# Two slots of modulation products in every second head, and one turn of their four rows

## The chip, the cores and the metric

The kernel runs on one core of a Trainium2 chip. Its time is the device time of one execution in microseconds, the median of several runs. The engines run side by side and meet at semaphores only: TensorE multiplies, VectorE (DVE) and ScalarE (ACT) work element by element and take results out of PSUM, GpSimd (POOL) takes a part of the element-wise work, and SyncE (SP) issues the transfers from the chip's memory, which 16 DMA engines carry out.

## The reference

256 tokens of width 1024, in fp32, pass through two blocks one after the other:

```
first block:  x += pool_mixer(rmsnorm(x));                     x += swiglu(rmsnorm(x))   # FFN1
              x += attention(rmsnorm(x), 16 heads of 64) @ w_o; x += swiglu(rmsnorm(x))  # FFN2
              x  = rmsnorm(x)
second block: mod = silu(c) @ ada_w + ada_b          # one row of 1024 times 1024 x 6144
              sh1, sc1, g1, sh2, sc2, g2 = split(mod, 6)
              h  = rmsnorm(x) * (1 + sc1) + sh1;  x += g1 * (mixed(h) @ w_out)
              h2 = rmsnorm(x) * (1 + sc2) + sh2;  x += g2 * moe_ffn(h2)
              x  = rmsnorm(x)
```

`mixed` joins a sparse attention of 8 heads and a recurrent branch; `moe_ffn` has 64 experts of width 256. The change bears on how `mod` is computed. It depends on the input `c` alone, so it can be done anywhere ahead of the second block; the kernel does its products inside the 16 heads of the first attention.

## The kernel before, in words

The program is one stream of instructions for each engine, written out by hand. Activations lie with features on partitions, as 8 chunks of 128 x 256 tokens. All weights but the experts' come as 93 slots of 128 x 3072 fp32 (1.5 MB) through a ring of 11 places in SBUF. SP loads slot n (L443 to L469; in this stretch L457) once the semaphore `w_used` says that the slot that had its place eleven before has been used. It issues in the order of the slots, on one queue. Slots 0 to 21 belong to FFN1, 22 to 29 to keys, values and queries (`S_KVQ`), 30 to 45 to the modulation (`S_ADA`), 46 to 48 to the output projection (`S_O`), 49 to 70 to FFN2 (`S_FFN2`).

**First attention** (`attention`, L610, on TensorE). Iteration j does the scores of head j (L618, L619), turns the softmax weights of head j-2 for the product with the values (L625, three transposes), calls `between(j)`, and multiplies the values of head j-3 (L635, L636). DVE adds the bias to the scores and takes the maximum (L1473 to L1480), ScalarE takes the exponential (L1142, L1143), DVE divides (L1485 to L1487), ScalarE copies the turned weights out of PSUM (L1150), and after every second head the result (L1154). On DVE the scores of head j come before the division of head j-1.

**Modulation** (`modulation`, L654). `between` is `modulation`: in each of the 16 heads it waits for one slot (128 rows of `ada_w` by 3072 columns) and does its six products of one column of silu(c) with 512 columns (L661). The 6144 results lie as twelve pieces of 512 in PSUM banks 5 to 7, four pieces in a bank, in rows 0, 32, 64 and 96: piece j is in bank 5 + j // 4, row 32 * (j % 4), and `tile_position=(0, r)` puts its matmul on the strip of 32 columns of the array that writes there. A fp32 matmul is two passes and shows as two records. Pieces add up over eight chunks of `c`, which are two slots each.

**Output projection** (L705): 64 matmuls of 128 x 256, 128 records. Then the **turning**. ScalarE has copied the four rows to SBUF (`modrow`), each by a copy of its own (L1208). 48 matmuls with one row of one element as the moving operand (L718) turn them, so that feature n of `mod` lies on partition n % 128. The sum of squares for FFN2's norm (`norm_sum(3)`, L558) stands after the second row of four. ScalarE then takes the root (L1105) and DVE the reciprocal (L1431); DVE adds `ada_b` to the turned columns (`modulation_columns`, L1566), and this releases TensorE (`mod_ready`) to clear FFN2's banks (L564) and to start FFN2 (L579 to L581). While the turning goes on, DVE and ScalarE add the last parts of the projection to x, split them into two parts each (L1100, L1101, L1429), and take their squares (L1102).

**The rest**: FFN2, the projections and branches of the second block (with a second attention of 8 heads by the same function, without `between`), and the experts, whose weights come by 64 loads of 3 MB.

Of the kernel before, what the change touches and what calls it, by code (L numbers as in the profile page):

```python
# [11 lines left out]
ALU = mybir.AluOpType  # L12
ACT = mybir.ActivationFunctionType
# [4 lines left out]
P = 128  # L18
# [6 lines left out]
HEADS_1, HEADS_2, HEAD = 16, 8, 64  # L25
# [52 lines left out]
VEC = {}  # L78
# [63 lines left out]
def build(nc, xT, vec, consts, selector, inv_count, pool_w, ws, rel, lora, router, router_bias, experts, out):  # L142
# [3 lines left out]
    with ExitStack() as ctx:  # L146
# [11 lines left out]
        vecs = sb("vecs", [P, N_VEC])  # L158
        con = sb("con", [P, N_CONST])
        ones = sb("ones", [P, P])  # L160
# [4 lines left out]
        mod = sb("mod", [P, 48])  # L165
# [226 lines left out]
        O2_PARTS, RW_PARTS, MIXED_PARTS = 5 * KC, 5 * KC + AC, 6 * KC  # L392


        def mod_products(q):
            return B[(4, 5, 0, 7)[q]][:, 0:12]

        PROJ_BANKS = [B[4], B[5], B[7]]
        U_V1, U_K1, U_Q1 = 0, 8, 16
# [149 lines left out]
        def _(pe):  # L549
# [3 lines left out]
            def norm_sum(k, bank=B[6], weights=lambda c: ones[:]):  # L553

                for g in range(4):
                    pe.wait_ge(sq_ready, SQ_BASE[k] + g + 1)
                    for c in (2 * g, 2 * g + 1):
                        mm = nc.tensor.matmul(bank[:, 0:T], weights(c), sq[:, c, :], start=(c == 0), stop=(c == KC - 1))  # L558
                mm.then_inc(ss_ready, 1)
# [94 lines left out]
            def modulation(n):  # L654
# [7 lines left out]
                                          skip_group_check=True, tile_position=(0, r))  # L662
                mm.then_inc(w_used, 1)


            pe.wait_ge(const_loaded, 16)
            norm_sum(2)
# [27 lines left out]
            pe.sem_inc(w_used, 8)  # L695
            pe.wait_ge(proj_used, U_Z)
            pe.wait_ge(csil_ready, 1)
            attention(HEADS_1, 0, q1, k1, v1, ex, pts, B[4:5], between=modulation)
            pe.wait_ge(o_copied, HEADS_1 // 2)
            for i in range(24, 32):  # L700
                dc = i - 24
# [6 lines left out]
            pe.wait_ge(res_ready, 4)  # L708
            pe.sem_inc(w_used, 3)

            pe.wait_ge(mod_copied, 4)
            for q in range(4):
                if q == 2:
                    norm_sum(3)
                for j in range(3):
                    for t in range(4):
                        row = slice(32 * q, 32 * q + 1)
                        mm = nc.tensor.matmul(mod_products(q)[:, 4 * j + t:4 * j + t + 1], modrow[row, j, t * P:(t + 1) * P], ones[row, 0:1], start=True, stop=True)  # L718
            mm.then_inc(mod_turned, 1)

            pe.wait_ge(mod_ready, 1)
            ffn(S_FFN2, 3, FFN_CHUNKS)
# [362 lines left out]
        def _(act):  # L1085
# [118 lines left out]
            attention(HEADS_1, 0, h, ex, pts, B[4:5])  # L1204

            act.wait_ge(w_used, S_O)
            for q in range(4):
                nc.scalar.activation(modrow[32 * q:32 * q + 1, :, :], banks[32 * q:32 * q + 1, 5:8, :], ACT.Copy).then_inc(mod_copied, 1)  # L1208
            ffn_start(S_FFN2)
            norm_squares(3, "norm_ffn1")  # L1210

# [185 lines left out]
        def _(dve):  # L1397
# [67 lines left out]
            def attention(heads, n0, bias, extra, ex):  # L1465
                for j in range(heads + 1):
                    if j < heads:
                        b, e, k = B[j % 2], ex[:, j % 3, :], 2 * (j % 3)
                        dve.wait_ge(s_ready, n0 + j + 1)

                        if j >= 3:
                            dve.wait_ge(pt_ready, n0 + j - 2)
                        nc.vector.scalar_tensor_tensor(e[:, 0:T], b[:, 0:T], HEAD ** -0.5, bias[:, j, :], ALU.mult, ALU.add)  # L1473
                        m = nc.vector.scalar_tensor_tensor(e[:, T:T + P], b[:, T:T + P], HEAD ** -0.5, bias[:, j, P:T], ALU.mult, ALU.add)
                        m.then_inc(s_used, 1)
                        dve.wait_ge(s_used, n0 + j + 1)
                        if extra is not None:
                            then(nc.vector.tensor_tensor(e, e, extra, ALU.add))
                        nc.vector.tensor_reduce(nmax[:, k:k + 1], e[:, 0:T], AX_X, ALU.max, negate=True)
                        nc.vector.tensor_reduce(nmax[:, k + 1:k + 2], e[:, T:T + P], AX_X, ALU.max, negate=True).then_inc(max_ready, 1)  # L1480
                    if j >= 1:
                        a = j - 1
                        e, k = ex[:, a % 3, :], 2 * (a % 3)
                        dve.wait_ge(exp_ready, n0 + a + 1)
                        then(nc.vector.reciprocal(rrec[:, k:k + 2], rsum[:, k:k + 2]))  # L1485
                        nc.vector.tensor_scalar(e[:, 0:T], e[:, 0:T], rrec[:, k:k + 1], None, ALU.mult)
                        nc.vector.tensor_scalar(e[:, T:T + P], e[:, T:T + P], rrec[:, k + 1:k + 2], None, ALU.mult).then_inc(p_ready, 1)  # L1487
# [78 lines left out]
            def modulation_columns():  # L1566
                dve.wait_ge(mod_turned, 1)
                by_row = lambda a: a.rearrange("p (j q t) -> p j q t", j=3, q=4)
                for q in range(4):
                    ins = nc.vector.tensor_tensor(by_row(mod[:])[:, :, q, :], mod_products(q).rearrange("p (j t) -> p j t", j=3), by_row(vecs[:, VEC["ada_b"][0]:VEC["ada_b"][1]])[:, :, q, :], ALU.add)  # L1570
                ins.then_inc(mod_ready, 1)
                dve.wait_ge(mod_ready, 1)
                for dst, col, g in ((scale1, 8, "norm1_g"), (scale2, 32, "norm2_g")):
                    last = nc.vector.scalar_tensor_tensor(dst[:], mod[:, col:col + 8], 1.0, vecs[:, VEC[g][0]:VEC[g][1]], ALU.add, ALU.mult)
                then(last)
# [437 lines left out]
```

## Time and profile before

| | us |
|---|---|
| median of 3 runs (lowest, highest) | 1533.23 (1532.24, 1540.92) |
| the profiled execution's own time | 1534.7 |
| its span in the profile | 1533.0 |
| TensorE busy, share of the span | 1420.4, 93% |
| VectorE busy | 718.2, 47% |
| ScalarE busy | 500.4, 33% |
| GpSimd busy | 171.5, 11% |
| DMA mean over the span | 236 GB/s |

The span is cut into 40 slices of 38.3 us. The first attention starts at 318 us, in the ninth slice, and FFN2 at 428, in the twelfth. In the slices from the ninth to the twelfth the page gives 280, 424, 395 and 95 GB/s of transfers. The modulation products are 192 matmul records at L661, the turning 96 at L718. A busy share says how long an engine had work in it, not that this work set the end; for that one reads the chain of waits, followed back from the last instruction, and then each stretch by itself.

### The profile page before, as it was taken

What the parts mean: (1) busy time and instruction counts of PE and PEld (TensorE: products, weight loads), DVE (VectorE), ACT (ScalarE), POOL (GpSimd) and SP (SyncE); (2) the same over time, 40 slices, a digit from 0 to 9 for tenths busy, and PEclk for the clock granted to TensorE, in tenths of its full rate; (3) what the DMA queues carried; (4) which work ended last, traced back from release to release, by engine and by line L of the source; (5) the groups of instructions that cost most, each with busy time, mean ns of one, the idle gap of its engine ahead of it and who ended that gap; (6) DMA issues with size and microseconds to landing.
All of it is one profiled execution on the core that took longest, in us unless ns stands there. A gap on an engine that the chain in (4) does not pass through costs nothing.

```text
span 1533.0 us, 25786 instructions
## 1 busy us (share of the span) xinstructions
PE 1420.4 (93%) x10983; PEld 1109.9 (72%) x10986; DVE 718.2 (47%) x1188; ACT 500.4 (33%) x809; POOL 171.5 (11%) x76
## 2 busy tenths in 40 slices
PE   4999997999999999799798877979999999999996
PEld 3999997954899999698695877845554545555453
DVE  5766656444266665689894537331112112211213
ACT  2533324434333342456334133221222222222221
POOL 0000000000000000376670024300000000000000
PEclk7999999999999999899896998889999999999998
DMA  9754552269925445113305042429889999999990
GB/s 362 312 201 165 179 191 83 56 280 424 395 95 190 181 168 199 44 43 125 120 5 247 3 167 83 173 99 396 342 343 407 426 425 425 422 424 426 420 376 28
DMA packets 36166, 362.16 MB, mean 236 GB/s; under 512 B 3955, under 2 KB 5107, under 8 KB 7412
## 3 DMA queue, kind: packets, MB, share of 16 engines
q1 hardware_dynamic: 35364, 358.50, 58.5%
q0 software_dynamic: 720, 2.46, 0.8%
q8 instruction: 65, 1.06, 0.3%
q14 instruction: 17, 0.14, 0.0%
HBM read 358.25 MB, written 2.69 MB: 235 GB/s over the span
## 4 chain that ended last, share of the span: by engine, by line
PE 84%; DVE 13%; ACT 1%; issue 1%; DMA 0%; POOL 0%; DVEq 0%; SPq 0%; ACTq 0%
PE banks L1018 14%; PE banks L579 12%; PE banks L580 12%; PE banks L581 12%; PE banks L1047 7%; PE banks L978 4%; PE banks L986 4%; PE banks L558 2%; DVE scr L1640 2%; PE banks L661 2%; PE banks L705 2%; DVE ring L1629 1%; PE banks L844 1%; PE banks L635 1%; PE banks L618 1%
## 5 line engine op out<-in xcount | busy, mean ns | idle before, releaser
L1018 PE MATMUL banks<-ring,scr 128*64 128x512 f32 x1024 | 225.4, 593 | 0.7 <-ACT scr L1349 0.7
L579 PE MATMUL banks<-h_hi,gu_hi 128*128 128x256 f32 x704 | 200.0, 284 | 0.0
L580 PE MATMUL banks<-h_lo,gu_hi 128*128 128x256 f32 x704 | 199.5, 283 | 0.0
L581 PE MATMUL banks<-h_hi,slot_lo 128*128 128x256 f32 x704 | 199.4, 283 | 0.0
L1018 PEld LDWEIGHTS banks<-ring,scr 128*64 128x64 f32 x1024 | 73.1, 137 | 145.6 <-issue 144.7
L579 PEld LDWEIGHTS banks<-h_hi,gu_hi 128*128 128x128 f32 x704 | 135.5, 192 | 0.4 <-issue 0.3
L580 PEld LDWEIGHTS banks<-h_lo,gu_hi 128*128 128x128 f32 x704 | 135.4, 192 | 0.1
L581 PEld LDWEIGHTS banks<-h_hi,slot_lo 128*128 128x128 f32 x704 | 135.4, 192 | 0.0
L1888 DVE TENSOR_TENSOR out_lo<-banks,out_hi 128x512 fp32r<-128x512 f32 x64 | 44.2, 691 | 194.2 <-ACT out_hi L1375 194.2
L581 PE MATMUL banks<-slot_lo,slot_lo 128*128 128x256 f32 x416 | 118.9, 286 | 0.0
L1047 PE MATMUL banks<-ring,scr 128*64 128x512 f32 x512 | 116.9, 598 | 0.9 <-ACT scr L1369 0.9
L1876 DVE TENSOR_TENSOR scr<-banks,scr 128x256 f32<-128x256 f32 x32 | 13.6, 424 | 198.8 <-ACT scr L1362 198.8
L579 PE MATMUL banks<-act_hi,down_hi 128*128 128x256 f32 x352 | 99.9, 284 | 4.1 <-DVE slot_lo L1414 4.1
L1414 DVE TENSOR_TENSOR slot_lo<-ring,gu_hi 128x2048 fp32r<-128x2048 f32 x44 | 100.6, 2291 | 3.0 <-ACT gu_hi L1116 3.0
L580 PE MATMUL banks<-act_lo,down_hi 128*128 128x256 f32 x352 | 99.6, 283 | 0.0
L581 PE MATMUL banks<-act_hi,slot_lo 128*128 128x256 f32 x352 | 99.6, 283 | 0.0
L1128 ACT ACTIVATE scr<-scr 128x256 f32<-128x256 f32 x44 | 18.4, 418 | 240.1 <-DVE scr L1446 240.1
L517 POOL TENSOR_TENSOR slot_lo<-ring,win_hi 128x1024 fp32r<-128x1024 f32 x20 | 48.6, 2433 | 369.8 <-ACT win_hi L1218 369.8
L1362 ACT ACTIVATE scr<-banks 128x256 f32<-128x256 f32 x32 | 12.3, 383 | 209.9 <-PE banks L1018 209.9
L581 PEld LDWEIGHTS banks<-slot_lo,slot_lo 128*128 128x128 f32 x416 | 80.7, 194 | 0.0
L1116 ACT ACTIVATE gu_hi<-ring 128x2048 fp32r<-128x2048 f32 x42 | 79.5, 1898 | 3.2 <-PE banks L718 3.2
L1047 PEld LDWEIGHTS banks<-ring,scr 128*64 128x64 f32 x512 | 33.9, 136 | 60.1 <-issue 54.8
(381 smaller groups left out, 3150.0 us busy)
## 6 DMA issues: line engine op xcount, KB each, us to landing
ring<-ws SPq DMA_DIRECT2D x93, 1536.0 KB, 7.5
ring<-experts SPq DMA_DIRECT2D x64, 2048.0 KB, 10.2
ring<-experts SPq DMA_DIRECT2D x64, 1024.0 KB, 9.7
ring<-experts SPq DMA_DIRECT2D x1, 3072.0 KB, 11.4
scr<-bias_line POOLq DMA_DIRECT2D x4, 512.0 KB, 8.8
bias_line<-scr SPq DMA_DIRECT2D x1, 1536.0 KB
x<-xT SPq DMA_DIRECT2D x1, 1024.0 KB, 5.0
scr<-pool_w SPq DMA_DIRECT2D x1, 1024.0 KB, 7.7
```

Of the source, the lines that this page charges most:

```text
L517: nc.gpsimd.tensor_tensor(dst, src, hi.bitcast(F32), ALU.subtract).then_inc(win_w_lo, 1)
L558: mm = nc.tensor.matmul(bank[:, 0:T], weights(c), sq[:, c, :], start=(c == 0), stop=(c == KC - 1))
L579: nc.tensor.matmul(out, hi, move_hi, start=start, stop=False, skip_group_check=True)
L580: nc.tensor.matmul(out, hi, move_lo, start=False, stop=False, skip_group_check=True)
L581: return nc.tensor.matmul(out, lo, move_hi, start=False, stop=stop, skip_group_check=True)
L978: mm = nc.tensor.matmul(bank[:, c * 4 * CAP:(c + 1) * 4 * CAP], tok[:, tb, kc * P:(kc + 1) * P], pick[q % 2][:, tb, :], start=(n == 0 and ...
L986: mm = nc.tensor.matmul(B[c // 2][:, c % 2 * T:c % 2 * T + T], part[:, c * P:(c + 1) * P], spread[k % 2], start=False, stop=False, skip_gr ...
L1018: mm = nc.tensor.matmul(B[4][CAP * j:CAP * (j + 1), :], hs[:, c, CAP * u:CAP * (u + 1)], unit(u)[:, c * 512:(c + 1) * 512], start=(c == 0) ...
L1047: mm = nc.tensor.matmul(B[6 + half][CAP * j:CAP * (j + 1), :], act_pt[:, f, CAP * j:CAP * (j + 1)], unit(u)[:, lo:lo + 512], start=(f == 0 ...
L1116: nc.scalar.activation(dst, slot(base + s)[:, lo:hi], ACT.Copy).then_inc(signal, 1)
L1414: nc.vector.tensor_tensor(slot_lo[PLACE[base + s]][:, lo:to], slot(base + s)[:, lo:to], hi.bitcast(F32), ALU.subtract).then_inc(signal, 1)
L1888: ins = nc.vector.tensor_tensor(out_lo[part], B[6 + half], out_hi[part].bitcast(F32), ALU.subtract)
```

## The change

It does three things. `two_modulations` does nothing in even heads and the products of two slots, one after the other, in odd heads; since banks 5 to 7 are then copied with rows in them that no product writes, three matmuls with zeros fill them first. The four row copies on ScalarE become one, of partitions 0 to 96. The 48 turning matmuls become 12: each has 97 rows of 128 columns as weights and as moving operand the columns 0, 32, 64 and 96 of the identity, so that it picks four rows at once and writes four neighbouring columns of bank 4. The sum of squares comes after the turning, and one addition on DVE takes the place of four.

```diff
--- before.py
+++ after.py
@@ -392,8 +392,8 @@
         O2_PARTS, RW_PARTS, MIXED_PARTS = 5 * KC, 5 * KC + AC, 6 * KC
 
 
-        def mod_products(q):
-            return B[(4, 5, 0, 7)[q]][:, 0:12]
+        mod_products = B[4][:, 0:48].rearrange("p (j t q) -> p j q t", j=3, t=4)
+        mod_rows = slice(0, 3 * 32 + 1)
 
         PROJ_BANKS = [B[4], B[5], B[7]]
         U_V1, U_K1, U_Q1 = 0, 8, 16
@@ -662,6 +662,11 @@
                                           skip_group_check=True, tile_position=(0, r))
                 mm.then_inc(w_used, 1)
 
+            def two_modulations(head):
+                if head % 2:
+                    modulation(head - 1)
+                    modulation(head)
+
 
             pe.wait_ge(const_loaded, 16)
             norm_sum(2)
@@ -695,7 +700,9 @@
             pe.sem_inc(w_used, 8)
             pe.wait_ge(proj_used, U_Z)
             pe.wait_ge(csil_ready, 1)
-            attention(HEADS_1, 0, q1, k1, v1, ex, pts, B[4:5], between=modulation)
+            for b in range(5, 8):
+                nc.tensor.matmul(B[b], zeros[:, 0:P], zeros[:], start=True, stop=False, skip_group_check=True)
+            attention(HEADS_1, 0, q1, k1, v1, ex, pts, B[4:5], between=two_modulations)
             pe.wait_ge(o_copied, HEADS_1 // 2)
             for i in range(24, 32):
                 dc = i - 24
@@ -708,15 +715,12 @@
             pe.wait_ge(res_ready, 4)
             pe.sem_inc(w_used, 3)
 
-            pe.wait_ge(mod_copied, 4)
-            for q in range(4):
-                if q == 2:
-                    norm_sum(3)
-                for j in range(3):
-                    for t in range(4):
-                        row = slice(32 * q, 32 * q + 1)
-                        mm = nc.tensor.matmul(mod_products(q)[:, 4 * j + t:4 * j + t + 1], modrow[row, j, t * P:(t + 1) * P], ones[row, 0:1], start=True, stop=True)
+            pe.wait_ge(mod_copied, 1)
+            for j in range(3):
+                for t in range(4):
+                    mm = nc.tensor.matmul(mod_products[:, j, :, t], modrow[mod_rows, j, t * P:(t + 1) * P], ident[mod_rows, 0:P:32], start=True, stop=True)
             mm.then_inc(mod_turned, 1)
+            norm_sum(3)
 
             pe.wait_ge(mod_ready, 1)
             ffn(S_FFN2, 3, FFN_CHUNKS)
@@ -1204,8 +1208,7 @@
             attention(HEADS_1, 0, h, ex, pts, B[4:5])
 
             act.wait_ge(w_used, S_O)
-            for q in range(4):
-                nc.scalar.activation(modrow[32 * q:32 * q + 1, :, :], banks[32 * q:32 * q + 1, 5:8, :], ACT.Copy).then_inc(mod_copied, 1)
+            nc.scalar.activation(modrow[mod_rows, :, :], banks[mod_rows, 5:8, :], ACT.Copy).then_inc(mod_copied, 1)
             ffn_start(S_FFN2)
             norm_squares(3, "norm_ffn1")
 
@@ -1566,8 +1569,7 @@
             def modulation_columns():
                 dve.wait_ge(mod_turned, 1)
                 by_row = lambda a: a.rearrange("p (j q t) -> p j q t", j=3, q=4)
-                for q in range(4):
-                    ins = nc.vector.tensor_tensor(by_row(mod[:])[:, :, q, :], mod_products(q).rearrange("p (j t) -> p j t", j=3), by_row(vecs[:, VEC["ada_b"][0]:VEC["ada_b"][1]])[:, :, q, :], ALU.add)
+                ins = nc.vector.tensor_tensor(by_row(mod[:]), mod_products, by_row(vecs[:, VEC["ada_b"][0]:VEC["ada_b"][1]]), ALU.add)
                 ins.then_inc(mod_ready, 1)
                 dve.wait_ge(mod_ready, 1)
                 for dst, col, g in ((scale1, 8, "norm1_g"), (scale2, 32, "norm2_g")):
```

## Rows read from the trace of the kernel before

**Rows 1.** The page, chain that ended last: shares of the span.
```profile
PE 84%; DVE 13%; ACT 1%; issue 1%; DMA 0%; POOL 0%; DVEq 0%; SPq 0%; ACTq 0%
```

**Rows 2.** Windows, TensorE: from:to length, busy (records), granted clock, DMA share, GB/s.
```profile
330.11:361.58 31.47, 31.47 (x186) 1.00 1.01 426
377.31:381.08 3.77, 3.68 (x23) 1.00 1.03 434
```

**Rows 3.** Chain of waits, one head: start, duration, engine, tile, line, count.
```profile
373.38 0.58 PE banks L635 x2
373.96 0.22 PE banks L636 x2
374.17 0.63 PE banks L618 x2
374.80 0.22 PE banks L619 x2
375.02 0.48 PE banks L625 x3
375.50 1.81 PE banks L661 x12
```

**Rows 4.** Timeline, TensorE's weight loads in one head: start, duration, [idle before].
```profile
325.09 0.10 PEld L661 LDWEIGHTS banks<-ring,small 128*1 128x1 f32 x8 [0.17 <-issue]
325.52 0.09 PEld L661 LDWEIGHTS banks<-ring,small 128*1 128x1 f32 x2 [0.33 <-issue]
...
326.90 0.29 PEld L618 LDWEIGHTS banks<-scr 64*128 64x128 f32 x2 [0.86 <-issue]
```

**Rows 5.** Line L457, slot loads: issue, and time to landing of first and last.
```profile
L457 SPq DMA_DIRECT2D ring<-ws x24: 332/333/2305, 318.2 to 377.5; - x24
...
DMA to landing us min/median/max: 7.8/7.8/7.8
...
DMA to landing us min/median/max: 33.3/33.3/33.3
```

**Rows 6.** Timeline, DVE in one head: scores taken up, last scaling.
```profile
327.86 0.42 DVE L1473 SCALAR_TENSOR_TENSOR scr<-banks,scr 128x256 f32<-128x256 f32 x1 [1.21 <-PE banks L619]
...
329.50 0.28 DVE L1487 TENSOR_SCALAR scr<-scr,small 128x128 f32<-128x128 f32 x1
```

**Rows 7.** Timeline, row copies on ScalarE and the output projection.
```profile
381.62 5.82 ACT L1208 ACTIVATE scr<-banks 1x1536 f32<-1x1536 f32 x4
...
381.77 27.89 PE L705 MATMUL banks<-scr,ring 128*128 128x256 f32 x128 [0.47 <-ACT scr L1154]
```

**Rows 8.** Chain of waits, from the projection's end to FFN2.
```profile
409.82 5.07 PE banks L718 x48
414.88 5.33 PE banks L558 x16
...
425.35 0.41 DVE mod L1570 x4
...
426.21 1.48 PE banks L564 x3
```

**Rows 9.** Windows, TensorE, columns as in group 2: the two falls of the clock.
```profile
414.96:418.37 3.41, 3.41 (x9) 0.50 1.01 425
425.20:428.61 3.41, 2.44 (x10) 0.50 0.00 0
```

**Rows 10.** Timeline, last square on ScalarE, reciprocal on DVE.
```profile
413.42 0.61 ACT L1102 ACTIVATE scr<-x 128x512 f32<-128x512 f32 x1
...
420.76 1.75 DVE L1431 RECIPROCAL rinv<-rt 128x256 f32<-128x256 f32 x1 [6.33 <-ACT rt L1105]
```

**Rows 11.** Windows, TensorE: a gap later in the kernel and what followed.
```profile
854.60:857.70 3.10, 0.01 (x2) 1.00 0.00 0
858.70:862.10 3.40, 3.40 (x71) 0.50 0.02 5
```

**Rows 12.** Windows, TensorE: a stretch of the second attention.
```profile
825.00:838.00 13.00, 12.70 (x38) 0.50 0.36 152
```

## The prediction, written before the result was known

> **What bounds the kernel now.** I read the chain of waits first: TensorE holds 84% of it [rows 1], and around the change all of it. The change touches the stretch from 318 us, where the first attention starts, to 428 us, where the second feed-forward (FFN2) is under way, so I read that stretch closely: first as windows, then head by head.
>
> In the windows TensorE is never idle while the heads run, at full granted clock, while the 16 DMA engines are as busy as they can be: share 1.01, 426 GB/s [rows 2]. So two resources are full at once, and an edit that relieves only TensorE gets only what the DMA lets through.
>
> The chain shows one head: values 0.58 + 0.22, scores 0.63 + 0.22, turning the weights 0.48, modulation 1.81 us [rows 3], a period of 3.93 us. Modulation is 46% of it. Its weight loads start in a burst of eight, then after 0.43 us a pair, and one more pair as much later [rows 4]. Each 1x512 fp32 matmul is two passes; four matmuls on the four column strips share the array. Six matmuls in one slot are thus a wave of four and a wave of two, at two passes of about 0.43 us each: 4 x 0.43 = 1.71, plus 0.10 before the array is free.
>
> The weights arrive on a schedule of their own. After 318.2 us 24 slots are issued; the first (modulation slot 3, since 0 to 2 were already there) lands after 7.8 us, at 326.0, the 24th (issued 377.5) after 33.3 us, at 410.8 [rows 5]. That is 84.8 / 23 = 3.69 us a slot, for demand every 3.93. Slot 15 is the 13th: 326.0 + 12 x 3.69 = 370.3 us, and before it is wanted at 375.5 [rows 3].
>
> **The change, part by part.**
>
> *Two slots in one place.* Twelve matmuls on four strips are three full waves: 6 x 0.43 + 0.10 = 2.67 us in place of 2 x 1.81 = 3.62. Two heads then need 2 x (0.80 + 0.85 + 0.48) + 2.67 = 6.93 us on TensorE in place of 7.86. Is anything else late first? The scores' matmuls begin at 326.90 [rows 4]; DVE takes them up 0.96 us later, at 327.86, and has then scaled the weights of the head before by 329.50 + 0.28 = 329.78 [rows 6], 2.88 us after the matmuls' start. In the new even-to-odd step TensorE comes to the turning of the weights 0.85 + 0.48 + 0.80 + 0.85 = 2.98 us after the even head's scores began; DVE is ready at 2.9. It just fits. Only in the first pair, where there are no values yet, does TensorE wait some 0.7 us.
>
> TensorE alone: scores of heads 0 and 1 after the new zero matmuls end at 320.8, first pair to 323.5, scores, turning, scores, the 0.7 us wait and turning to 326.9; six more periods bring the last pair to 326.9 + 6 x 6.93 = 368.5, its end to 371.1. From the end of the last modulation to the output projection it is 381.77 - 377.31 = 4.46 us [rows 3, 7]; start at 375.6.
>
> The DMA: two slots need 7.38 us, more than 6.93. From the fourth pair on the odd slot is late, and its six matmuls then run alone. For the last: 370.3 + 1.8 + 4.5 = 376.6. The later of the two counts, **376.6 instead of 381.8: 5.1 us won** (6.2 if the DMA did not bind). The projection's own slots land at 374.0, 377.7 and 381.4, each before its use (the third of its 27.9 us [rows 7] begins 21 us in). Slots are given back up to 2.9 us later, but eleven are outstanding, so the queue stays full. The three issues that wait for the projection's end come while the queue still drains, and FFN2 has eight slots in hand by then.
>
> *Zeros into banks 5 to 7.* Three 128x512 bf16 matmuls. The nearest row is the same form before FFN2: the stretch of 1.48 us at half clock [rows 8, 9], so about 0.2 us each at full clock, 0.65 in all (at most 1.5). It is on TensorE's path, but lies before the stretch in which the DMA sets the pace; that covers it. Without this cover it costs the 0.65 that I put into the 375.6.
>
> *One row copy.* ScalarE's four copies hold 381.62 to 387.44 [rows 7]; one is a quarter, since only the partitions are more. 4.4 us less, hidden beside the projection: it only has to precede its end. Worth nothing. The split of FFN2's first slot comes after it, but waits for a slot that lands at 326.0 + 16 x 3.69 = 385.0.
>
> *Turning in twelve matmuls.* Before: 48 records (24 matmuls of two passes) in 5.07 us, twice, with the sum of squares (5.33) between them [rows 8]. One record is 0.106 us. Now 24 records. No row has 97 rows and four moving columns; below stands 0.106 (1 row, 1 column), above 0.16 (turning the weights, 128 rows and 128 moving columns, 0.48 / 3 [rows 3]): 2.5 to 3.8 us. I take 2.5, as four columns are far nearer to one than to 128. The Trainium skill (TensorEngine Tiling, Instruction Overhead) says a matmul with one moving column lasts as long as one with sixty; that would give the same 2.5, and no run here shows it.
>
> *The sum of squares comes last.* Counted from the projection's end (409.68): turning ends at +2.7. The last square is written at 414.03 = +4.35 [rows 10]; the three parts ahead of it take till +5.3, so it isn't waited for. At full clock 16 records of 0.218 (the projection's 27.9 / 128 [rows 7], same shape) are 3.5 us: end at **+6.2, before +10.5**. But the reciprocal, which lay beside the second turning, is now on the path. After the sum: the reciprocal starts 0.54 later (420.76 after 420.21) and takes 1.75 [rows 10]; then one addition of 0.2 in place of 0.41, and 0.45 till the first clearing matmul (426.21 after 425.76) [rows 8]: TensorE idles **2.9 us** and begins to clear at +9.1 (before +16.5). FFN2's second slot is split by ScalarE and DVE beside its first, as before.
>
> *The clock.* Before, the granted clock fell from its upper level to half (2.4 to 1.2 GHz) after five microseconds of turning, at 415, for about 3.4 us, and again at the end of the second turning [rows 9]. The first made the sum of squares 1.9 us longer, the second the clearing 0.7 (1.48 against 0.75) and FFN2, which began at 427.69, 0.5. Now turning is short, but 2.9 us of idleness follows. A gap of 3.10 us elsewhere was followed, a microsecond after work resumed, by 3.4 us at 0.50 [rows 11]: 1.7 us lost. Without a fall FFN2 runs at full rate from +9.85 against an effective +18.5: 8.6 won. With it: 6.9, with a longer one 5.2. I take **7.3**, between.
>
> **Sum**: 5.1 + 7.3 = 12.4 us. The profiled execution took 1534.7 (span 1533.0 and 1.7 around it); 1522.3 there. The median of the runs shown is 1533.2, 1.5 lower: 1520.8, so 1521. What follows FFN2 is started by TensorE's or DVE's progress and moves along.
>
> **The rivals.**
>
> *A, the waves don't cross the slots.* If the wait or the semaphore between two slots keeps the second's matmuls out of the half-full wave, a pair costs 3.62, and the zeros and the first wait lie open: the projection starts at 383.2, 1.4 us later than before. With the turning: 12.4 - 6.5 = 5.9 won, 1527. For it: no burst in the trace crosses a slot. Against it: with the slot landed, nothing in between holds the queue, and records go out four at a time [rows 4].
>
> *B, neither DMA nor clock takes its part.* 6.2 + 8.6 = 14.8, 1518.4. For it: the gap is 2.9, shorter than the one that was followed by a fall. Against it: the landings are counted and stood in queue throughout.
>
> *C, slower: the clock falls during attention.* Even steps have no modulation any more; 4.3 us of scores, turning and values lie between pairs, in place of 2.1. The second attention, which has none at all, ran at 0.50 for 13 us on end [rows 12]. If the first falls to half in an even step and stays there, a pair costs 13.9 instead of 7.86, 8 x 6.0 = 48 us more, with the turning gain left: 1534.7 + 48 - 7.3 - 1.5 = 1574. Two pairs at half eat up the gain; from about four on the kernel is over 1% slower (12.4 + 15.3 = 27.7, at 13.9 - 7.4 = 6.5 each). Against it: 3.77 us without modulation at the end of attention kept 1.00 [rows 2], and with it the granted clock stayed up into the projection. The Trainium skill (TensorE: Matmul & The Clock Gate, Part 4: PE-mode transpose) has it that transposes don't count as work for the clock; by that rule the even steps are poorer still than they look. The trace shows that they suffice for 3.8 us.
>
> **Numbers.** Forecast 0.63, A 0.12, B 0.2, C 0.05. The range takes in A and B and the spread of the clock: 1516.5 to 1528; the forecast alone 1518.5 to 1523.5. A measurement of this kernel can tell 1% (15.3 us) from nothing; 1517.9 is the line. The far side of B passes it, a bit over half of its 0.2: faster 0.12. Slower: C, 0.05. Same: 0.83.
>
> **What would show it.** After: eight groups of 24 modulation records, the first three 2.67 us long, and from the fourth on 1.81 twice with a gap before the second that ends with a landing; the projection's start near 376.6; turning x24 in 2.5; the sum of squares in 3.4; then 2.9 us idle for the reciprocal. Wrong if the pair takes 3.6, if the projection starts after 379, if the granted clock in the heads is below 1.00, or if FFN2 starts less than 6 us closer to the projection's end.

## The result, and the profile after

The kernel before and the changed one ran in turn on one chip, eleven executions each. The medians are 1531.73 us (1530.4 to 1540.92) and 1527.82 us (1520.37 to 1532.45); the ratio is 0.9945, 95% interval 0.9926 to 0.9964. That is faster, by less than 1%, and 6.8 us above the forecast of 1521. The two profiled executions say something else: 1534.7 before, 1523.15 after (span 1521.5), 11.55 us apart where the forecast had 12.4. Two gaps are to be explained: 12.4 against 11.55, and 11.55 in the profiles against 3.9 between the medians. In what follows, "a profile" is the one profiled execution of a run, and a run's own time is the median of its executions.

The stretches, from one first matmul to the next (us):

| | before | after | won | forecast |
|---|---|---|---|---|
| start to the first scores | 318.44 | 318.04 | 0.4 | 0 |
| first scores to projection | 63.33 | 57.35 | 6.0 | 5.1 |
| projection to FFN2 | 45.36 | 40.02 | 5.3 | 7.3 |
| FFN2 to the last instruction | 1105.90 | 1106.07 | -0.2 | 0 |

The shares of the chain of waits hardly move against [rows 1]:

```profile
PE 83%; DVE 14%; ACT 1%; issue 1%; DMA 0%; DVEq 0%; SPq 0%; ACTq 0%
```

**The heads.** The chain of waits of the kernel after, two heads in place of the one of [rows 3] (start, duration, engine, tile, line, count; the second head's values, scores and turning left out):

```profile
340.55 2.69 PE banks L661 x24
343.24 0.58 PE banks L635 x2
343.81 0.22 PE banks L636 x2
344.03 0.63 PE banks L618 x2
344.66 0.22 PE banks L619 x2
344.88 0.48 PE banks L625 x3
...
347.47 2.69 PE banks L661 x24
```

Twenty-four records take 2.69 us, and the period of a pair is 6.92. The weight loads of such a pair, from the timeline of TensorE's loads (start, duration, line, shape, count, [idle before]), against [rows 4]:

```profile
340.48 0.10 PEld L661 LDWEIGHTS banks<-ring,small 128*1 128x1 f32 x8 [0.17 <-issue]
340.91 0.10 PEld L661 LDWEIGHTS banks<-ring,small 128*1 128x1 f32 x4 [0.33 <-issue]
341.34 0.10 PEld L661 LDWEIGHTS banks<-ring,small 128*1 128x1 f32 x4 [0.33 <-issue]
```

After the first eight, four come every 0.43 us, where before they were two: the second slot's matmuls take the places that the first slot's last wave leaves empty.

**From the projection to FFN2**, the chain of waits after, against [rows 8]:

```profile
403.29 0.14 issue
403.43 2.81 PE banks L721 x24
406.24 5.26 PE banks L558 x16
...
411.53 0.48 ACT rt L1109
...
412.03 1.76 DVE rinv L1434
...
413.82 0.22 DVE mod L1572
414.04 0.45 issue
414.49 1.49 PE banks L564 x3
```

TensorE clears at +11.2 us from the projection's end (403.29), not at +9.1. The line of L558 shows why: the sum of squares takes 5.26 us, almost what it took before. The windows of TensorE (from:to, length, busy and records, granted clock, DMA share, GB/s) give the reason, and two windows of the heads beside them:

```profile
324.90:328.30 3.40, 3.40 (x18) 0.50 1.00 426
330.00:361.00 31.00, 31.00 (x203) 1.00 1.01 426
406.80:410.20 3.40, 3.40 (x9) 0.50 1.00 417
413.60:417.00 3.40, 2.52 (x9) 0.50 1.02 430
```

The clock falls to half (1.2 GHz) 0.6 us after the sum of squares begins, for 3.4 us, and again before the clearing: two falls, as before [rows 9]. It also fell once in the heads, and then stayed up.

**The row copy** on ScalarE, from its timeline, against [rows 7]: a quarter, as counted, and beside the projection.

```profile
375.23 1.44 ACT L1211 ACTIVATE scr<-banks 97x1536 f32<-97x1536 f32 x1
```

### The profile page after: what moved, and what is told of

Its sections match the earlier page's. It is cut to its first block, busy times and chain, and to the rows that moved or that the text cites. A ratio compares the mean times of both kernels' runs of the same rounds, so it can differ in the third digit from the quotient of the medians.

```text
span 1521.5 us, 25641 instructions
## 1 busy us (share of the span) xinstructions
PE 1406.1 (92%) x10913; PEld 1100.9 (72%) x10917; DVE 720.0 (47%) x1185; ACT 495.3 (33%) x806; POOL 171.6 (11%) x76
## 3 DMA queue, kind: packets, MB, share of 16 engines
HBM read 358.25 MB, written 2.69 MB: 237 GB/s over the span
## 4 chain that ended last, share of the span: by engine, by line
PE 83%; DVE 14%; ACT 1%; issue 1%; DMA 0%; DVEq 0%; SPq 0%; ACTq 0%
PE banks L1022 14%; PE banks L579 12%; PE banks L581 12%; PE banks L580 12%; PE banks L1051 8%; PE banks L982 4%; PE banks L990 4%; DVE scr L1642 2%; PE banks L558 2%; PE banks L712 2%; PE banks L661 2%; DVE ring L1631 1%; PE banks L848 1%; PE banks L635 1%; PE banks L569 1%
## 5 line engine op out<-in xcount | busy, mean ns | idle before, releaser
L579 PE MATMUL banks<-h_hi,gu_hi 128*128 128x256 f32 x704 | 200.0, 284 | 0.0
L581 PE MATMUL banks<-h_hi,slot_lo 128*128 128x256 f32 x704 | 199.4, 283 | 0.0
L579 PEld LDWEIGHTS banks<-h_hi,gu_hi 128*128 128x128 f32 x704 | 135.5, 193 | 0.4 <-issue 0.3
L581 PEld LDWEIGHTS banks<-h_hi,slot_lo 128*128 128x128 f32 x704 | 135.4, 192 | 0.0
L581 PE MATMUL banks<-slot_lo,slot_lo 128*128 128x256 f32 x416 | 118.9, 286 | 0.0
L579 PE MATMUL banks<-act_hi,down_hi 128*128 128x256 f32 x352 | 99.9, 284 | 4.1 <-DVE slot_lo L1417 4.1
L581 PE MATMUL banks<-act_hi,slot_lo 128*128 128x256 f32 x352 | 99.6, 283 | 0.0
L581 PEld LDWEIGHTS banks<-slot_lo,slot_lo 128*128 128x128 f32 x416 | 80.7, 194 | 0.0
```

The source lines that it names most:

```text
L579: nc.tensor.matmul(out, hi, move_hi, start=start, stop=False, skip_group_check=True)
L581: return nc.tensor.matmul(out, lo, move_hi, start=False, stop=stop, skip_group_check=True)
```

## The experiments

The expectations of the first runs speak of theories by number. Theory 1: the spread of the changed kernel's times is the clock in the heads. Theory 2: it arises after FFN2 begins. Theory 3, formed after the third run: it is code that TensorE has to fetch again, ahead of everything that the change touches.

In the diffs below `...` stands for lines left out.

**e1_pairs**: the pairs alone, on the kernel before.

```diff
+            def two_modulations(head):
+                if head % 2:
+                    modulation(head - 1)
+                    modulation(head)
...
-            attention(HEADS_1, 0, q1, k1, v1, ex, pts, B[4:5], between=modulation)
+            attention(HEADS_1, 0, q1, k1, v1, ex, pts, B[4:5], between=two_modulations)
```

> The kernel before with the two slots in every second head and nothing else (no zeros, four row copies, 48 turning matmuls). Both theories: a pair of slots in 2.67 us where the second slot has landed, the projection's start near 376, so 5 to 6 us less in the profiled execution: 1527 against a median of 1532. Theory 1 (the wide spread of the changed kernel, 1520 to 1532, comes from the granted clock, which falls in the heads without modulation in a part of the executions): this kernel shows the spread too, some executions hardly under 1531, and a fall of the clock between 318 and 375 in the profile or none at all, as it comes. Theory 2 (the spread comes from something after FFN2 starts, set off by the earlier start of FFN2): about half of the spread or none.

Measured: 1529.67 us, 12 executions (1523.6 to 1536.82), ratio 0.9976 [0.9956, 0.9997]. In its profile (1523.6) the projection starts 58.04 us after the first scores, 5.3 less than before. Here the landings can be seen to set the pace. Groups of modulation records in its chain, the fifth to the seventh:

```profile
345.20 3.14 PE banks L661 x24
...
352.58 3.12 PE banks L661 x24
...
359.94 3.14 PE banks L661 x24
```

Their starts lie 7.37 us apart, two slots at 3.69, not 6.92. And within one such group, TensorE's weight loads:

```profile
359.87 0.10 PEld L661 LDWEIGHTS banks<-ring,small 128*1 128x1 f32 x8 [0.17 <-issue]
360.30 0.09 PEld L661 LDWEIGHTS banks<-ring,small 128*1 128x1 f32 x2 [0.33 <-issue]
360.73 0.09 PEld L661 LDWEIGHTS banks<-ring,small 128*1 128x1 f32 x2 [0.34 <-issue]
361.20 0.10 PEld L661 LDWEIGHTS banks<-ring,small 128*1 128x1 f32 x6 [0.38 <-DMA ring<-ws]
```

The first slot's last wave goes on with two records at a time, since the second slot isn't there; then a landing releases the rest. The clock did not fall in these heads.

**e2_turn**: the changed kernel with the old distribution over the heads (the zeros stay).

```diff
-            attention(HEADS_1, 0, q1, k1, v1, ex, pts, B[4:5], between=two_modulations)
+            attention(HEADS_1, 0, q1, k1, v1, ex, pts, B[4:5], between=modulation)
```

> The changed kernel with one slot in each head, as before the change; zeros, one copy, twelve turning matmuls and the late sum of squares stay. The projection starts near 382.3 (0.6 for the zeros), FFN2 starts 12.7 us after its end in place of 18.0: 1527 in the profiled execution. Theory 1: executions close together, within 2 us, like the kernel before. Theory 2: spread over 8 us like the changed kernel.

Measured: 1529.71 us, 12 executions (1523.75 to 1538.46), 0.9975 [0.9951, 0.9999]. The spread is as wide without the pairs, so theory 1 falls. In its profile heads to projection take 63.33 us, the time of before to the hundredth, and projection to FFN2 39.89. The chain after the projection:

```profile
416.14 2.81 PE banks L721 x24
418.95 5.26 PE banks L558 x16
```

The turning's gain and the slow sum of squares are there whatever happens in the heads. The two parts add up: 5.3 (e1_pairs) and 5.5 (45.36 - 39.89) are 10.8 of the 11.3 that both stretches win in the profile of after.

**e3_repeat**: the changed kernel once more, nothing edited.

> The changed kernel once more, word for word, to see another of its executions: 1520 to 1532. Theory 1: where the profiled execution takes 1527 or more, its clock is at half for more than 3.4 us between 318 and 375; where it takes 1521, for less. Theory 2: the stretch from 318 to FFN2's start is the same within 1 us in both and the difference of 5 us lies behind it.

Measured: 1521.38 us, 6 executions (1518.39 to 1530.22), 0.9912 [0.9884, 0.994]. The profile caught the 1530.22. Neither theory held: heads 57.05, projection to FFN2 40.03, both as in the other profile. The difference is that its first scores come at 325.35 us and not at 318.04. The windows of TensorE in FFN1, first after (1523.15), then e3_repeat:

```profile
139.00:144.00 5.00, 5.00 (x44) 1.00 0.85 332
144.00:149.00 5.00, 5.00 (x44) 1.00 0.12 49
```

```profile
139.00:144.00 5.00, 0.43 (x2) 0.68 0.85 292
144.00:149.00 5.00, 4.79 (x26) 0.64 0.31 124
```

and the place where e3_repeat stands still, in its timeline of TensorE:

```profile
138.45 0.28 PE L581 MATMUL banks<-act_hi,slot_lo 128*128 128x256 f32 x1
143.56 0.55 PE L579 MATMUL banks<-h_hi,gu_hi 128*128 128x256 f32 x1 [4.84 <-issue]
```

TensorE stands 4.84 us for "issue", which is no wait on another engine, exactly where FFN1's loop branches back to its first instruction (L581 to L579). Then the clock is at half for a few microseconds. The page's section on DMA queues has the missing piece, packets, MB and share, first after, then e3_repeat:

```profile
q8 instruction: 65, 1.06, 0.3%
```

```profile
q8 instruction: 74, 1.21, 0.3%
```

Nine packets more of code, 0.15 MB, and 7.3 us to the first scores. And these nine lie in the loop's second turn. The DMA view of e3_repeat for 122 to 234 us has this line:

```profile
q8 instruction: 9, 0.15, 0.6%
```

The same view of after has no packet on queue q8. Two of the nine fall between 138 and 144 us, where TensorE stands still, the other seven in the turn after it. That is theory 3. Of the profiles so far, e2_turn (1533.63) has 74 packets and a standstill of 5.41 us at the same branch; before, after and e1_pairs have 65 and none.

Read with this, the times of the changed kernel fall into two groups: after and e3_repeat together have ten executions between 1518.39 and 1524.98, median 1521.65, and seven from 1527.82 to 1532.45, median 1528.33. The kernel before, over 62 executions on four chips (those of all runs up to e10_after_unroll), has 39 up to 1534.1 with a median of 1531.36 and 23 from 1535.89 with 1538.2. Group against group the change is worth 9.7 and 9.9 us. On the fifth chip, that of e11_before_unroll_again and e12_before_unroll_two, its 23 executions go from 1528.55 to 1542.24 without an empty stretch between (four lie from 1535.16 to 1535.43), so for the kernel before the border between the groups is not a sharp one.

**e4_bank7**: the turned columns go to bank 7, which FFN2 doesn't use at first, so TensorE no longer waits for DVE's addition before it clears and starts FFN2.

```diff
-        mod_products = B[4][:, 0:48].rearrange("p (j t q) -> p j q t", j=3, t=4)
+        mod_products = B[7][:, 0:48].rearrange("p (j t q) -> p j q t", j=3, t=4)
...
-            pe.wait_ge(mod_ready, 1)
             ffn(S_FFN2, 3, FFN_CHUNKS)
+            pe.wait_ge(mod_ready, 1)
```

> The changed kernel with the turned columns in bank 7 in place of 4, and TensorE's wait for mod_ready behind FFN2 instead of ahead of it. FFN2 no longer waits for the reciprocal and the addition: 2.9 us of idleness go, and with it one fall of the clock may go. Expected 3 us under the changed kernel on the same chip, up to 5 if the clock stays up; 0 if the wait is taken over by another (the split of the last part of x, DVE's L1432, ends before).

Measured: 1518.66 us, 6 executions (1517.15 to 1527.71), 0.9909 [0.9877, 0.9941]; the profile is of the 1517.15. Heads 57.31, projection to FFN2 36.61, 3.4 less than after. The chain:

```profile
403.25 2.81 PE banks L721 x24
406.06 5.25 PE banks L558 x16
411.31 0.86 PE banks L564 x4
412.17 0.12 PE banks L579
```

The gap of 3.0 is gone, and with it the second fall (clearing 0.86, FFN2's first record 0.12 in place of 0.21). The first fall stays: 5.25. So the gap for the reciprocal does not bring about the slow sum of squares: the first fall comes without the second.

**e5_order**: e4_bank7, and the twelve turning matmuls stand in the middle of the sum of squares.

```diff
-            def norm_sum(k, bank=B[6], weights=lambda c: ones[:]):
+            def norm_sum(k, bank=B[6], weights=lambda c: ones[:], midway=None):
...
+                    if g == 2 and midway is not None:
+                        midway()
...
-            norm_sum(3)
+            norm_sum(3, midway=turn_rows)
```

> The kernel with the turned columns in bank 7, and the twelve turning matmuls put between the second and the third part of the sum of squares, where TensorE would else wait for the squares. Theory a (it is the low work of 2.8 us of turning in one piece right ahead of the sum that costs the clock): from the projection's end to the end of the sum 6.3 us in place of 8.2, no fall there, 1.9 us less than with bank 7 alone. Theory b (any such turning costs the clock wherever it stands): the fall stays, the time is that of bank 7 within 0.5 us.

Measured: 1522.78 us, 6 executions (1513.85 to 1524.58), 0.9894 [0.9863, 0.9926]. The profiled 1522.7 is one of the upper group (74 packets, a standstill of 5.54 us at FFN1's branch), but its stretch can be read: projection to FFN2 34.93, another 1.7 less. Chain, then the window of TensorE:

```profile
412.11 1.97 PE banks L560 x8
414.08 2.58 PE banks L724 x24
416.65 1.83 PE banks L560 x8
418.49 0.05 issue
418.54 0.81 PE banks L566 x3
```

```profile
411.80:420.00 8.20, 8.00 (x51) 1.00 1.01 425
```

The same work, 40 records, takes 6.38 us in place of 8.07, without a fall. That this is the doing of the order is likely, but the next run takes from the proof.

**e6_half**: of each of the 16 modulation slots only half is loaded, and the products use that half twice, so half of `ada_w` is left out. TensorE's work is the same. (The slot number has to be known ahead for this, so three turns of SP's loop of slot loads are written out.)

```diff
-                    sp.dma_start(slot(s), ws[RING * i + s]).then_inc(landed[s], 16)
+                    n = RING * i + s
+                    cols = SLOT // 2 if isinstance(i, int) and S_ADA <= n < S_O else SLOT
+                    sp.dma_start(slot(s)[:, 0:cols], ws[n][:, 0:cols]).then_inc(landed[s], 16)
...
-                    mm = nc.tensor.matmul(B[5 + j // 4][r:r + 1, :], csil[:, c:c + 1], w[:, b * 512:(b + 1) * 512], start=(c == 0), stop=(c == KC - 1),
+                    mm = nc.tensor.matmul(B[5 + j // 4][r:r + 1, :], csil[:, c:c + 1], w[:, b % 3 * 512:(b % 3 + 1) * 512], start=(c == 0), stop=(c == KC - 1),
```

> The changed kernel with half of each modulation slot loaded and used (columns 0 to 1535 twice; the other half of ada_w is left out). Theory of the forecast (from the fourth or fifth pair on the second slot's landing sets the pace): no group of modulation records lasts more than 2.7 us, all eight pairs come every 6.92 us, from the first scores to the projection 56.3 us at full clock in place of 57.3. Rival (TensorE, DVE or the code sets the pace there and the landings only coincide): groups of 3.05 us every 7.38 us stay, 57.3.

Measured: 1523.28 us, 6 executions (1521.7 to 1525.64), 0.9915 [0.9891, 0.9939]. Its profile (1524.93) has the 74 packets and a standstill of 5.34 us at FFN1's branch, so the whole time says little; the stretch is what counts. Every group takes 2.69 and they come 6.92 apart to the end. Two of them, late in the chain:

```profile
354.36 2.69 PE banks L669 x24
...
361.28 2.69 PE banks L669 x24
```

Heads to projection 55.71, against 57.05 to 57.43 in seven profiles with the whole loads: the transfers cost the change 1.6 us. In this profile the clock did not fall in the sum of squares:

```profile
410.31 2.81 PE banks L729 x24
413.13 3.57 PE banks L566 x16
...
419.51 0.81 PE banks L572 x3
```

```profile
410.30:420.00 9.70, 6.86 (x44) 1.00 0.89 341
```

So 3.57 us is the price at full clock. The second fall did not come either: TensorE stood idle for 2.82 us ahead of the clearing, which then took 0.81, and the window from the turning to FFN2 has 1.00 throughout (projection to FFN2 37.70). With turning first the fall is likely, not certain: it is in six profiles of seven (after, e2_turn, e3_repeat, e4_bank7, e7_unroll, e10_after_unroll). Turning and sum of squares take 6.38 us here as well, as in e5_order. So two profiles with the other order and no fall (e5_order, e8_both) are in favour of the order, but one profile without it had none either, and the order is not shown to be the cause. What else differed in e6_half, the halved loads or the moment at which the stretch came, no run separates.

**e7_unroll**: the changed kernel, with TensorE's loop of FFN1 written out, so that nothing branches back there.

```diff
-                with pe.Fori(0, 2) as i:
+                def turn(i):
...
+                if k == 1:
+                    turn(0)
+                    turn(1)
+                else:
+                    with pe.Fori(0, 2) as i:
+                        turn(i)
```

> The changed kernel with FFN1's loop of two turns on TensorE written out (no branch back; the same matmuls in the same order). Theory 3 (in two fifths of the executions of every version, before the change too, TensorE fetches the loop's code a second time near 138 us and stands still for it; that makes the spread): the upper group near 1528 to 1530 is gone, all executions within 1519 to 1525, and the profile shows no gap near 138 us. Rival (the gap has another cause, such as the transfers of that moment): still two groups, 7 us apart.

Measured: 1523.15 us, 6 executions (1521.45 to 1525.94), 0.9918 [0.9895, 0.9942]. One group (its highest 0.9 above the expected band), and no standstill near 138 us, as theory 3 had it; heads 57.40, projection to FFN2 40.02.

**e8_both**: e5_order and e7_unroll together.

> Order, bank 7 and the written-out loop together. If theory 3 and theory a hold: median 1516, all within 1514 to 1520; with theory 3 and b: 1518; with neither: median 1518 and an upper group at 1525.

Measured: **1516.17 us**, 6 executions (1515.36 to 1517.32), **0.9868 [0.9845, 0.9891]**. Heads 57.27, projection to FFN2 34.93. Sum of squares and turning take 1.97, 2.58 and 1.83 us in its chain, the numbers of e5_order, so there was no fall here either. It is the best version, ahead of both kernels, and its spread is 2 us where the changed kernel's is 14.

**e9_before_unroll** and **e10_after_unroll**: e7_unroll's edit on the kernel before, and e7_unroll again, side by side, so that the change is read without the two groups.

> The kernel before the change with FFN1's loop on TensorE written out and nothing else. Theory 3 (the upper group of executions, present before the change too, is the loop's code fetched again): one group within 1530 to 1535, no execution at 1536 or more. Rival (the kernel before has its upper group from something else): two in five executions at 1536 or more.

> The changed kernel with the same loop written out, beside the kernel before treated the same, so that the change is measured without the second fetch: 10 to 11.5 us less (6 in the heads, 5.3 from the projection to FFN2, less where the clock falls elsewhere). Were the gain of the profiled executions given back later, the two would lie less than 8 us apart.

Measured: e9_before_unroll 1533.1 us, 12 executions (1528.76 to 1541.3), 1.0004 [0.998, 1.0029]; five are at 1537.92 and more. e10_after_unroll 1522.51, 6 executions (1521.49 to 1524.67), 0.9919 [0.9892, 0.9946]; its profile has both falls, heads 57.43 and projection to FFN2 40.02. Theory 3 in its narrow form, that only FFN1's loop loses its code, failed in the kernel before. Against e9_before_unroll's seven lower ones (median 1530.94) the change is worth 8.4 us, less than the expected 10 to 11.5.

**e11_before_unroll_again**: e9_before_unroll, for a profile of one of its upper executions.

> The kernel before with FFN1's loop written out once more, for a second profile: 5 of its 12 executions were at 1538 to 1541 although no code of FFN1 can be fetched twice. If the profiled execution is an upper one, theory 3 in its wider form (any of TensorE's loops over a feed-forward can lose its code) has it that the gap of 5 us stands where FFN2 branches back, near 525 us, with nine packets of 16 KB more on the instruction queue than the 72 of the lower one. Rival: the gap is elsewhere, with 72 packets.

Measured: 1532.72 us, 8 executions (1528.09 to 1539.71, three at 1538.29 and more), 1.0001 [0.9974, 1.0028]. The profiled execution was a lower one (72 packets), so this run shows nothing about where the upper ones lose their time.

**e12_before_unroll_two**: the kernel before, the loops of FFN1 and FFN2 both written out.

```diff
-                if k == 1:
-                    turn(0)
-                    turn(1)
-                else:
-                    with pe.Fori(0, 2) as i:
-                        turn(i)
+                turn(0)
+                turn(1)
```

> The kernel before with the loops of both FFN1 and FFN2 on TensorE written out. Theory 3 in its wider form: one group, all executions within 1529 to 1535. Rival: two in five still at 1536 or more.

Measured: 1531.92 us, 12 executions (1530.48 to 1533.51), 0.9985 [0.9972, 0.9998]. All twelve lie within about 3 us, while six of the 23 of the kernel before on that chip are at 1537.3 or more. In the wider form, that each of these loops can lose its code, theory 3 holds so far: with neither loop the upper group is gone. Longer code is then fetched in every execution (78 packets in the profile), and TensorE does not stand still for it.

## Why the prediction was right or wrong

Most of the chance lay on a change of less than 1%, and that was right. That the range held the time, by 0.2 us, is luck: six executions of eleven lost some 7 us at a place that the forecast did not know, and the median is the lowest of these six. The mechanism came as forecast but for one stage, the clock between projection and FFN2. In the profiles 12.4 became 11.55 by four parts: 2.0 less in that stage, 0.9 more in the heads, 0.4 more ahead of the scores, 0.2 less behind FFN2's start. Step by step:

**Two slots in one place: right.** A pair was to take 2.67 us and takes 2.69. Rival A is dead: the waves do cross the slots, in every profile with pairs. The odd slot was to be late from the fourth pair on, with two loads at a time before a landing; e1_pairs shows that to the row. In the profile of after it is hidden, for a chance reason: TensorE had waited 0.7 us for DVE in the first step, as counted, the clock fell right after for 3.4 us (the wait is in all profiles with pairs, the fall in this one alone), the second pair took 4.27 in place of 2.69, and by that delay the slots were there in time. Only one landing was waited for, for 0.2 us. Both ways end the same: six other profiles with the whole loads have 57.05 to 57.43, and the odd slot late from the fifth or sixth pair on. That is what it means that the transfers set the pace. e6_half gives the bound its price, 1.6 us, where the forecast had 1.0.

The forecast 5.1 came out as 5.3 in e1_pairs and as 6.0 after. Of the 6.0, about 0.7 is the zeros: they delay the first scores, but not the first slot's issue (317.1 us, 1.0 ahead of the scores, [rows 5]: 0.2 ahead), so the transfers start with a lead. Counted from that issue it is 5.2 after, too (63.53 to 58.31).

**Zeros and row copy: right.** From the first issue to the projection it is 58.2 us in e1_pairs, which has no zeros, and 58.3 in after, which has them: the transfers cover them. The copy takes 1.44 us beside the projection.

**Turning: nearly right.** 2.81 for the forecast 2.5, within 2.5 to 3.8: a record of four moving columns and 97 rows comes every 0.111 to 0.117 us, against 0.106 [rows 8].

**The sum of squares: wrong, and this is the step that failed.** "At full clock 16 records of 0.218 are 3.5 us" was sized for a clock that wasn't granted. It measured 5.26. The forecast had read from [rows 8, 9] that the clock falls after five microseconds of turning, and concluded "Now turning is short". In six profiles of seven it fell after 2.8 us of turning just as well, and it struck the sum of squares as before (5.33). In after, behind it, the gap of 3.0 (forecast 2.9) went with a second fall, as [rows 11] let expect; in e6_half a gap of 2.8 did not. The stage was priced between none and one such fall; there were two. From 9.85 us to the measured 12.7 the terms are 1.8 for the sum, 0.7 for the clearing, 0.25 for the turning and 0.1 for the gap. The first two are the clock. That they are the clock is shown by the same 40 records at 1.00, 6.38 us in e5_order and e6_half against 8.07. What brings the fall is less sure: with eight records of the sum of squares on either side of the turning it is gone in two profiles of two, with turning first in one of seven. In e4_bank7 the gap is gone and the second fall with it, while the first stays. The Trainium skill (TensorE: Matmul & The Clock Gate, Part 4: PE-mode transpose) has it that transposes don't count as work for the clock. It says so of the transpose mode; the twelve matmuls of the turning are ordinary ones with columns of the identity, so the rule doesn't cover them as it stands. Six falls behind them look alike to it, and e6_half, where they ran alone and 1.00 stayed, does not. The even heads, which turn the softmax weights by transposes, brought no fall in the window 330 to 361 us, but these stand between other matmuls there; no run isolates them.

**Rival B** (14.8 us, neither DMA nor clock) did not come: the clock took its part in after, and the transfers in the other profiles with whole loads. **Rival C** came in miniature and without harm: one fall in the heads in one of nine profiles with pairs. It never stayed down.

**The median.** The forecast carried the gain of one profiled execution over to "the median of the runs shown" as if the times were one thing. They are two groups. Some executions lose about 7 us near 139 us, long before the first instruction that the change touches. One of before's three times shown ahead (1540.92) was of that size, and could have been taken for a second group. Six of the changed kernel's eleven were, so their median, 1527.82, is the lowest of its upper group, set against before's 1531.73 from its lower one: 3.9 us. The ratio of the whole comparison says 8.4 (5.5 to 11.3). Group against group it is 9.7 and 9.9; with the loop written out, against e9_before_unroll's lower executions, 8.4. These are 1.6 to 3.1 us less than the pair of profiles shows, and 2.5 to 4 less than the forecast. A part of that is the start: 1533.2, from which the forecast counted, is 1.9 above the lower group of the kernel before (1531.36). So e3_repeat's 1521.38, next to the forecast 1521, is no proof of its sum. The rest can't be read from a pair of profiles: FFN2 to the last instruction varies from 1100.1 (e1_pairs) to 1106.1 (e3_repeat) among them, with the time at half clock in it, 91.8 us in the first and 104.6 in the second.

**What stays open.** No upper execution of the kernel before was caught in a profile, so that its slower executions are FFN1's or FFN2's code is inferred from e9_before_unroll and e12_before_unroll_two, not seen. Why writing out FFN1 alone suffices in the changed kernel (18 of 18 executions in e7_unroll, e8_both and e10_after_unroll) and not in the kernel before (8 of 20 upper) isn't known. Why e6_half escaped both falls isn't either, and with it what the order of e5_order does for the clock stays likely, not shown.

## What to carry to other kernels

Packing work into column strips that stood empty pays at once, until the transfers bind: so count the landings beside the engine, and price the bound as soon as both are near full. When a stretch shows a clock fall, don't count on it to go because the light work ahead of it gets shorter: here it stayed in six profiles of seven. Dense work on both sides of the light work is worth a try (no fall in two of two), and so is taking out of the way what TensorE waits for, which won 3.4 us in e4_bank7. And before a gain of under 1% is measured, look at the times one by one: if they come in two groups, compare profiles of both until the place where they part is known, which can lie far ahead of the edit.

## What was not expected of the hardware

The code of a loop on TensorE can be fetched a second time, for its second turn. Then the branch back costs 4.84 us in e3_repeat (5.34 to 5.54 in e2_turn, e5_order and e6_half), with nine instruction packets of 16 KB more (74 for 65), and the half clock behind it brings this to 7.3 us. It happens in some executions of the same program and not in others. Written out, e8_both spreads over 2 us, and e12_before_unroll_two over 3.

Twenty-four matmuls of four columns, one every 0.11 us, show as 2.81 us of unbroken work, and yet in six profiles of seven the granted clock fell to half 3.3 to 4.0 us after their start, in the dense matmuls behind them. Those paid for it, not the turning. In the seventh, e6_half, it stayed at full, and so it did in e5_order and e8_both, where the sum of squares' records stand before and behind the same 24.
